# Five more pairs of projections as seven block products, between the heads of a hybrid decoder step

## The reference

```python
h = rmsnorm(x, norm1_w)
proj = jnp.einsum('btd,de->bte', h, w_in)
u_pool, u_qkv, b_raw, a_raw, z, gate_pool, gate_delta = jnp.split(proj, SPLITS, axis=-1)
y_pool, pool_buf_new = pool_mix(u_pool, pool_buf, pos0, w_pool, pool_scale)
qkv, conv_buf_new = causal_conv(u_qkv, conv_buf, w_conv)      # conv_buf_new: last 3 rows of u_qkv
# in gated_delta_chunked, for each head and chunk:
decay = jnp.exp(jnp.where(causal, G[..., :, None] - G[..., None, :], -jnp.inf))
A = jnp.einsum('bnhid,bnhjd->bnhij', kb, k) * decay * strict
t_inv = lax.linalg.triangular_solve(eye + A, ...)              # unit lower triangular
a_qk = jnp.einsum('bnhid,bnhjd->bnhij', q, k) * decay
# and after it:
o = rmsnorm(o, o_norm_w) * jax.nn.silu(z)
merged = jax.nn.sigmoid(gate_pool) * branch_pool + jax.nn.sigmoid(gate_delta) * branch_delta
```

## Time and profile before

| | |
|---|---|
| median of 3 runs | 568.15 us (567.43 to 569.66) |
| the profiled execution | 569.31 us, of which its span 567.5 us |
| TensorE busy | 528.8 us (93%) |
| VectorE, ScalarE, GpSimd busy | 291.0 (51%), 155.6 (27%), 166.1 us (29%) |
| HBM traffic | 277 GB/s over the span; 419 to 424 GB/s from about 370 to 540 us |

### The profile page before, as it was taken

How to read it: one execution, slowest core, us unless ns; L and a number is a source line. 1 busy time by engine, 2 the same in 40 slices (tenths; PEclk the granted TensorE clock), 3 DMA queues, 4 the chain that set the end, 5 groups by cost and what they waited for, 6 DMA issues and landing times.

```text
span 567.5 us, 13134 instructions
## 1 busy us (share of the span) xinstructions
PE 528.8 (93%) x5276; PEld 409.9 (72%) x5276; DVE 291.0 (51%) x843; ACT 155.6 (27%) x415; POOL 166.1 (29%) x247
## 2 busy tenths in 40 slices
PE   7999999999999999999999999999999949699983
PEld 6899999977777787998899888657455425365442
DVE  3877667683645848456756344533524411405044
ACT  3258466414862012233100124210011101010114
POOL 6687678113051199644033222000000000000001
PEclk9999999999999999999999999999999969889999
DMA  9835454566982138694479898899999999999992
GB/s 264 238 102 155 147 162 150 180 208 230 319 226 79 11 99 264 195 304 131 154 236 366 335 423 314 345 424 419 421 419 420 419 422 422 419 419 422 422 364 86
DMA packets 81375, 158.03 MB, mean 278 GB/s; under 512 B 11182, under 2 KB 65083, under 8 KB 69251
## 3 DMA queue, kind: packets, MB, share of 16 engines
q1 hardware_dynamic: 76572, 153.56, 73.7%
q10 hardware_dynamic: 4743, 3.64, 2.5%
HBM read 149.40 MB, written 7.96 MB: 277 GB/s over the span
## 4 chain that ended last, share of the span: by engine, by line
PE 73%; DMA 11%; SPq 6%; DVE 4%; issue 4%; ACT 1%; ACTq 0%; DVEq 0%
PE ps L1552 14%; PE ps L1545 12%; DMA arena<-in_w_up_dram 8%; PE ps L1874 6%; PE ps L2265 5%; PE ps L2119 5%; PE ps L2071 5%; SPq L733 4%; PE ps L2175 3%; PE ps L1498 3%; PE ps L2326 3%; PE ps L2026 2%; DMA arena<-in_w_down_dram 2%; PE ps L2346 2%; PE ps L2172 1%
## 5 line engine op out<-in xcount | busy, mean ns | idle before, releaser
L1545 PE MATMUL ps<-arena 128*128 128x288 f32 x320 | 81.4, 409 | 0.7 <-DVE arena L2516 0.7
L1552 PE MATMUL ps<-arena 128*128 128x144 f32 x616 | 78.3, 287 | 0.0
L1552 PEld LDWEIGHTS ps<-arena 128*128 128x128 f32 x616 | 76.3, 190 | 2.4 <-issue 1.9
L2265 PE MATMUL ps<-arena 128*32 128x256 f32 x1024 | 63.1, 403 | 14.8 <-DMA arena<-in_w_up_dram 13.0
L1545 PEld LDWEIGHTS ps<-arena 128*128 128x128 f32 x320 | 59.7, 190 | 17.2 <-issue 1.7
L2265 PEld LDWEIGHTS ps<-arena 128*32 128x32 f32 x1024 | 36.6, 116 | 39.3 <-issue 23.0
L997 POOL TENSOR_TENSOR arena<-arena 128x512 f32<-128x512 f32 x2 | 2.5, 1274 | 204.4 <-ACT arena L1458 204.4
L2541 DVE SCALAR_TENSOR_TENSOR ps<-arena,ps 128x312 f32<-128x312 f32 x72 | 39.1, 545 | 2.2 <-ACT ps L1117 0.9
L1874 PE MATMUL ps<-arena 128*128 128x144 f32 x280 | 37.0, 290 | 0.3 <-issue 0.3
L1874 PEld LDWEIGHTS ps<-arena 128*128 128x128 f32 x280 | 34.9, 190 | 1.7 <-issue 1.4
L1498 PE MATMUL ps<-arena 128*128 128x128 f32 (+7 forms) x162 | 26.7, 284 | 7.2 <-DVE arena L3320 5.1
(11 more groups left out here) (453 smaller groups left out, 844.1 us busy)
## 6 DMA issues: line engine op xcount, KB each, us to landing
arena<-in_w_gate_dram SPq DMA_DIRECT2D x32, 1024.0 KB, 12.5
arena<-in_w_up_dram SPq DMA_DIRECT2D x32, 1024.0 KB, 17.7
arena<-in_w_down_dram SPq DMA_DIRECT2D x28, 1024.0 KB, 17.8
arena<-in_w_in_dram SPq DMA_DIRECT2D x26, 1024.0 KB, 5.7
out_dram<-arena SPq DMA_DIRECT2D x9, 512.0 KB, 5.3
arena<-in_w_branch_delta_dram SPq DMA_DIRECT2D x4, 1024.0 KB, 10.4
arena<-in_w_out_dram SPq DMA_DIRECT2D x4, 1024.0 KB, 5.4
arena<-in_state_delta_dram SPq DMA_DIRECT2D x7, 512.0 KB, 8.2
```

What stands on the lines that cost most here:

```text
L1545: last = mm(ps[n % 2][:, 0:T], w[:, k, P * (n % 2):P * (n % 2) + P], hT[:, k, :], start=(k == 0), stop=(k == KD - 1))
L1552: last = mm(to[:, 0:HT], left[:, k, :], right[:, k, :], start=(first and k == 0), stop=(k == HK - 1), skip_group_check=True)
L2265: last = mm(to[CAP * e:CAP * e + CAP, 0:FE], xgT[:, k, CAP * e:CAP * e + CAP], w[e][:, k, :], start=(k == 0), stop=(k == KD - 1))
```

## The change

- Items 15 to 18 (PREP_PAIRS) and 19 (LAST_PREP) are computed in blocks too. Between the heads TensorE does four blocks of a pair, `prep(h)`, three blocks, `prep(h + 1)`; the sample's small products are moved to the places that the diff shows. Only items 14 and 20 stay plain.
- VectorE's `prep` is cut into `prep_times`, `prep_decays` and `prep_products`, with the additions of the pair between them. Three additions of item 19 stand inside the substitution; `new_values` stands ahead of it.
- ScalarE evacuates z with Copy and takes one Silu over all of zT later. It makes the spread columns of the second set (`second_columns`) and copies the sums of the tokens for the last five pairs (`token_sums`) from those made at the start, which lie in gT; VectorE's `sum_tokens` goes. `rows_exp(0)` stands ahead of the copy of the pool rows.
- GpSimd sums the weights of the five new pairs, and of LEAD_PAIR, in halves; the first of them ahead of the clearing of X.
- SP: the decay rows are stored and read back ahead of the conv stores. Both are tied to item 17, which now goes to slot 0, as item 18 did. PAIR_A is loaded inside `diagonal_blocks`.
- Slots, semaphore counts and the buffers of the last stage are renumbered accordingly.

The diff, cut to its core:

```diff
-LATE_FAST = range(IN_ITEMS - 5, IN_ITEMS)
-LEAD_PAIR, PAIR_A, PAIR_B, PAIR_C, PAIR_D = LATE_FAST
+PLAIN = IN_ITEMS - 6
+PREP_PAIRS = range(PLAIN - 5, PLAIN - 1)
+LAST_PREP = PLAIN - 1
+LATE_FAST = (*PREP_PAIRS, LAST_PREP, *range(PLAIN + 1, IN_ITEMS))
...
-SLOT_OF = [i % 4 if i < NQKV // 2 else i % RA for i in range(LATE_FAST[0])] + [3, 4, 1, 2, 3, 1, 2, 4, 3, 0, 5, 1, 2, 4, 3]
-LATE_SUMMED, LATE_SUMS = 0, 5
+SLOT_OF = [i % 4 for i in range(NQKV // 2)] + [0, 1, 2, 3, 4, 0, 1, 2, 3, 4, 5, 2, 3, 4, 2, 3, 5, 4, 1, 0, 2, 3, 5, 4]
+LATE_SUMMED, PREP_SUMS, LATE_SUMS = 1, 5, 0
+SUMS_ORDER = (*FAST, *PREP_PAIRS, LEAD_PAIR, LAST_PREP, PAIR_A, PAIR_B, PAIR_C, PAIR_D)
...
-CONV_AT = NQKV // 2 + RA
-ROWS_AT = NQKV // 2 + RA
-DIAG_AT = LATE_FAST[1]
+CONV_AT = NQKV // 2 + RA - 1
+ROWS_AT = NQKV // 2 + RA - 1
+DIAG_AT = LEAD_PAIR
...
+                load_weights(PAIR_A)
...
-                if i == RA + 15:
+                if i == RA + 13:
                     sp.wait_ge(S["memsets"], 1)
                     sp.dma_start(x_image, X[:, 0:2 * H * TILE]).then_inc(S["diag"], 16)
+                if i == ROWS_AT:
+                    head_rows()
                 if i == CONV_AT:
                     store_conv()
...
+                behind = i in LATE_FAST and i not in (PREP_PAIRS[0], LEAD_PAIR)
+                if behind:
+                    pool.wait_ge(S["proj"], product(pair_ahead(i), L_P7))
+                elif i in LATE_FAST:
+                    s, v = item_read(reader_ahead(i, sums_slot(i)))
                     pool.wait_ge(s, v)
-                elif i in LATE_FAST:
-                    pool.wait_ge(S["proj"], product(i - 1, L_P7))
                 if i - 2 in FAST:
                     pool.wait_ge(S["proj"], product(i - 2, P4))
-                nc.gpsimd.tensor_tensor(s1, a21, a22, ALU.add).then_inc(S["pads"], 1)
+
+                def combine(to, a, b, op):
+                    if i in PREP_PAIRS or i in (LAST_PREP, LEAD_PAIR):
+                        link(nc.gpsimd.tensor_tensor(to[:, 0:2], a[:, 0:2], b[:, 0:2], op))
+                        to, a, b = to[:, 2:HK], a[:, 2:HK], b[:, 2:HK]
+                    nc.gpsimd.tensor_tensor(to, a, b, op).then_inc(S["pads"], 1)
+
+                combine(s1, a21, a22, ALU.add)
                 pool.wait_ge(S["pads"], weights_summed(i, 1))
-                nc.gpsimd.tensor_tensor(s2, s1, a11, ALU.subtract).then_inc(S["pads"], 1)
-                nc.gpsimd.tensor_tensor(s3, a11, a21, ALU.subtract).then_inc(S["pads"], 1)
+                combine(s2, s1, a11, ALU.subtract)
+                combine(s3, a11, a21, ALU.subtract)
                 pool.wait_ge(S["pads"], weights_summed(i, 2))
-                if i in LATE_FAST[1:]:
-                    pool.wait_ge(S["proj"], product(i - 1, L_P3))
-                nc.gpsimd.tensor_tensor(s4, a12, s2, ALU.subtract).then_inc(S["pads"], 1)
+                if behind:
+                    pool.wait_ge(S["proj"], product(pair_ahead(i), L_P3))
+                combine(s4, a12, s2, ALU.subtract)
...
+            sum_weights(PREP_PAIRS[0])
             nc.gpsimd.memset(X, 0.0).then_inc(S["memsets"], 1)
...
+            sum_weights(PREP_PAIRS[1])
             pool.wait_ge(S["diag"], 16)
             own_columns(0)
-            pool.wait_ge(S["sd_pe"], 1)
-            own_columns(1)
-            sum_weights(LATE_FAST[0])
+            sum_weights(PREP_PAIRS[2])
+            sum_weights(PREP_PAIRS[3])
+            sum_weights(LEAD_PAIR)
+            sum_weights(LAST_PREP)
...
-                    nc.scalar.activation(zT[:, n - N_Z, :], src[:, 0:T], ACT.Silu).then_inc(S["proj_free"], 1)
+                    nc.scalar.activation(zT[:, n - N_Z, :], src[:, 0:T], ACT.Copy).then_inc(S["proj_free"], 1)
...
+            rows_exp(0)
             act.wait_ge(S["stage_out"], 16 * 2 * (1 + BD))
...
+            for i in PREP_PAIRS:
+                h = 2 * (i - PREP_PAIRS[0])
+                late_first(i)
+                if h:
+                    rows_exp(h)
+                rows_exp(h + 1)
+                if h == 4:
+                    second_columns()
+                if h == 0:
                     act.wait_ge(S["decdve"], 1)
                     nc.scalar.activation(Dq, Dq, ACT.Exp).then_inc(S["dec_act"], 1)
-                evac(N_Z + Z_AHEAD + h)
-            evac(N_Z + Z_AHEAD + H)
+            act.wait_ge(S["sums"], late_added(PREP_PAIRS[2], L_SUM1))
+            nc.scalar.activation(zT, zT, ACT.Silu).then_inc(S["silu"], 1)
+            late_first(LAST_PREP)
             act.wait_ge(S["diag"], 16 * IMAGE_WRITES)
             for m in BY_SCALAR:
                 read_diagonal(act, m)
-            for n in range(N_GATE + 3, N_GATE + LEAD_GATES):
-                if n == N_GATE + LEAD_GATES - 1:
-                    act.wait_ge(S["sub_done"], 1)
-                    for m in BY_SCALAR:
-                        write_inverse(act, m)
-                evac(n)
+
...
+                act.wait_ge(S["proj"], product(PREP_PAIRS[3], L_P2))
+                at = HT * (3 * HK + 2)
+                flat_sums = summed.rearrange("p j k t -> p (j k t)")
+                nc.scalar.activation(room_l[:, 0:at], flat_sums[:, 0:at], ACT.Copy).then_inc(S["ht_done"], 1)
+                nc.scalar.activation(room_w, flat_sums[:, at:], ACT.Copy).then_inc(S["ht_done"], 1)
+
+            token_sums()
+            late_tanh(PREP_PAIRS[3])
+            late_tanh(LAST_PREP)
+            evac(2 * PLAIN)
+            evac(2 * PLAIN + 1)
+            late_first(LEAD_PAIR)
+            act.wait_ge(S["sub_done"], 1)
+            for m in BY_SCALAR:
+                write_inverse(act, m)
...
+            def late_products(i, between=nothing):
+
+                a11, a12, a22 = late_left(i)
+                s1, s2, s3, s4 = [weight_sums(i)[:, j] for j in range(4)]
+                behind_plain = i in (PREP_PAIRS[0], LEAD_PAIR)
+                pe.wait_ge(ring_in[SLOT_OF[i]], 16 * loads_in(SLOT_OF[i], i + 1))
+                if behind_plain:
+                    pe.wait_ge(S["proj_free"], free[2 * i - 2])
+                else:
+                    pe.wait_ge(S["sums"], late_added(pair_ahead(i), L_SUM1))
+                late_block(0, a11, lambda k: hT[:, k, 0:HT])
+                between()
+                pe.wait_ge(S["pads"], weights_summed(i, 2))
+                if behind_plain:
+                    pe.wait_ge(S["proj_free"], free[2 * i - 1])
+                if i == LEAD_PAIR:
+                    pe.wait_ge(S["ht_done"], late_summed_by(2))
+                late_block(1, s2, late_right(i, 1))
+                pe.wait_ge(S["proj_free"], late_free(i, 1))
+                late_block(0, s1, late_right(i, 0))
+                pe.wait_ge(S["pads"], weights_summed(i, 3))
+                pe.wait_ge(S["sums"], late_added(i, L_SUM2))
+                late_block(1, s3, late_right(i, 2))
+
+            def late_products_back(i):
+
+                a11, a12, a22 = late_left(i)
+                s4 = weight_sums(i)[:, 3]
+                pe.wait_ge(S["pads"], weights_summed(i, 4))
+                pe.wait_ge(S["sums"], late_added(i, L_SUM4))
+                late_block(0, s4, lambda k: hT[:, HK + k, HT:T], opens=False)
+                pe.wait_ge(S["sums"], late_added(i, L_SUM7))
+                late_block(1, a22, late_right(i, 3), opens=False)
+                pe.wait_ge(S["sums"], late_added(i, L_SUM5))
+                late_block(0, a12, lambda k: hT[:, HK + k, 0:HT])
...
-            for h in range(H):
-                proj(N_Z + Z_AHEAD + h)
+            for i in PREP_PAIRS:
+                h = 2 * (i - PREP_PAIRS[0])
+                late_products(i)
                 prep(h)
                 if h == 0:
                     sample_rows()
-                if h == 2:
+                if h == 4:
                     sample_tiles(2, 0, TS, Nq, lambda own, j: ident[own, own])
-                if h == 3:
+                    state_products(0)
+                if h == 6:
+                    sample_tiles(4, 0, TS, IAq, lambda own, j: N2q[own, j, :])
+                late_products_back(i)
+                prep(h + 1)
+                if h == 4:
                     sample_tiles(3, 2 * TS, TS, tq, lambda own, j: Nq[own, j, :])
-                if h == 4:
-                    sample_tiles(4, 0, TS, IAq, lambda own, j: N2q[own, j, :])
-                    state_products(0)
-                if h == 5:
+                if h == 6:
                     sample_flips()
-            proj(N_Z + Z_AHEAD + H)
             state_products(1)
-
-
-            for n in range(N_GATE + 3, N_GATE + LEAD_GATES):
-                proj(n)
-                if n == N_GATE + 3:
-                    sample_tiles(7, 0, P, TTq, lambda own, j: Rq[own, j, :])
-                if n == N_GATE + LEAD_GATES - 1:
-                    sample_tiles(8, 2 * P, P, aqq, lambda own, j: vnq[own, j, :])
+            late_products(LAST_PREP)
+            sample_tiles(7, 0, P, TTq, lambda own, j: Rq[own, j, :])
```

(50 more changed lines are left out.)

182 lines of the change are left out of this document (78 added, 104 removed).

## The result

The changed kernel takes 578.81 us, the median of four runs (575.27 to 580.00), against 568.22 (567.43 to 569.66) for the kernel before in the same session: 1.0173 of it (95% interval 1.0121 to 1.0225). So it is some 10 us slower. In a later session the same kernel took 577.05 us (574.62 to 578.87, four runs), 1.0132 of before (1.0091 to 1.0172), some 8 us. The forecast was 571.3, with a range to 575.5; slower was the likelier sign by a hair (0.47 against 0.46 for no change), and the size is outside in both sessions.

The account below looks back on a forecast made before the run. TensorE bounds the kernel to about 355 us, then expert weight loads, so front changes carry through. -4.0 - 0.5 + 3.1 + 2.1 + 2.3 = +3.0, +3.1 with semaphores, gave 571.3 us; range 567.2 to 575.5.

Parts of the forecast that it names:

- the decay rows ahead of the conv stores: Front: rows' store, landing and reads (2.53 us) delay the pool rows' copy; first block +3.1 us later (2.5 to 5.2).
- The windows: VectorE's windows ahead of head 0's exponentials, held by GpSimd's sums, end at about 133.9 instead of 131.14.
- the 1.8 us of the row of the copy: The moved memset may hold the windows' additions 1.8 us more; taken as nothing, left in the range.
- The clock: Rival: TensorE's 3 us standstill at 134 halves its clock, losing 2.0 us: 573.3; chance 0.19 shared with VectorE's loop.
- Seven products between the heads: Loop of the heads: VectorE's two-input steps, held by GpSimd's sums, cost +2.1 us in all (0.3 to 4.5).
- The saving: Five pairs in blocks of half width instead of plain on TensorE: 0.8 us each, -4.0 us (3.5 to 4.5).
- The rival in which the additions hide: VectorE's and GpSimd's instructions slip past each other in gaps; loop loses only 0.3 us; 568.0, not slower; chance 0.24.
- the one in which each held step costs 0.64 more: Rival: VectorE bounds the loop of the heads; with the memset's 1.8 us, 575.5; chance 0.19 shared with the clock.
- The rival in which nothing waits at the conv stores: Pool rows' copy doesn't follow the last conv store, so the 3.1 us go: 565.1 to 568; chance 0.07.
- Behind the last head: After the last head's products, TensorE waits for VectorE's additions inside the substitution: +2.3 us (1.0 to 3.5).
- the ended waits: TensorE's waits at 197.08 and just after, behind the substitution, end as new values move ahead: -0.5 us at most.
- The range's lower end: Whole kernel: 567.2 us, said to come from the lower ends of queue and loop together.

Follow-up runs that it names:

- rows_by_scalar: Changed kernel, decay rows stored and read back from ScalarE's DMA queue, head 0's exponentials behind the pool rows: 572.01 us, 1.0038 of the kernel before.
- no_sums: As rows_by_scalar, but GpSimd's weight sums of six pairs are made on 8 columns of one block only: 569.83 us, single run.
- combined: As rows_by_scalar, with PAIR_B's load moved ahead of the inverse's write-back and head 0's exponentials behind the first product's copy: 567.38 us, 0.9973 of the kernel before.
- rows_ahead_of_load: Changed kernel, SP stores and reads the decay rows one item earlier, ahead of item 17's load: 573.96 us, 1.0092 of the kernel before.
- whole_sums: As rows_by_scalar, but each GpSimd sum is one 128 x 512 instruction, not two halves: 574.98 us, 1.0093 of the kernel before.
- before_rows_first: Kernel before, with only the decay rows stored and read back ahead of the conv stores: 579.15 us, 1.0187 of the kernel before.
- exp_behind: Changed kernel, only head 0's exponentials on ScalarE moved behind the pool rows: 577.54 us, 1.0148 of the kernel before.
- after_again: Changed kernel unaltered, run once more for a second profile, which is of a run of 578.87 us.

## Why the prediction was wrong

**The failed step: the decay rows ahead of the conv stores.** The mechanism was right: the copy of the pool rows follows the last conv store, there is no slack, and TensorE stands idle ahead of the third pool product. The size was not: +3.1 was forecast, 5.2 at most, and it was +6.8 in the first profile and 6.95 in the second. The step took store, landing and reads as 2.53 us from where they stood, and moved that price along. But there the store followed the conv stores, 18 KB each, and landed after 1.70; in its new place it follows a 1 MB load on the same queue. Copy to copy it is 138.76 less 131.92, less the 1.05 of the later start: 5.79, of which 2.53 were counted and 3.26 are the landing. The other 1.01 is the pool's product at half the clock. The Trainium skill (DMA: Bandwidth & Descriptors, Queues, rings and completion order) says that an engine takes the descriptors of one issuer's ring in order and alternates between rings. By it a small store behind a large load on SP's ring waits for that load; the landings of 4.9 and 6.8 behind loads against 2.4 without one agree. That a store on ScalarE's ring would not wait isn't shown: in rows_by_scalar it landed after 2.5, but it was issued at 114.21, ahead of that load.

**The windows** were a second bound in that step, and set too high. They were to end at 133.9; they ended at 133.41 in after, 132.36 without the later start. The moved memset ran beside the additions for 0.8 us and didn't hold them:

```profile
128.85 1.80 POOL L905 MEMSET arena<- 128x2048 f32 x1
129.85 2.47 DVE L2790 TENSOR_TENSOR arena<-arena 128x422 f32<-128x422 f32 x4
```

In no_sums the four additions take 2.48 with GpSimd idle. So the 1.8 us of the row of the copy were rightly left out of the sum. The rule of the Trainium skill that was weighed there (SBUF — State Buffer, Who interferes with whom), that a VectorE instruction with two SBUF inputs doesn't contend with a GpSimd instruction that only writes, agrees; the rows of copies that a memset did hold are of another kind of instruction.

**The clock.** It was a rival, priced at 2.0 and left out of the sum, and it came true. It cost 1.01 at the pool's product, inside the 6.8, and 1.39 in the first four blocks (5.47, against 4.08 in combined). The gap was 5.66 us where 3 were forecast; whether one of 3 would have done it no run shows, but one of 3.55 did, and so did four of the six waits of 1.80 to 2.11 us told of above. The Trainium skill (TensorE: Matmul & The Clock Gate, Part 1) has the fall follow from idleness and the return from work; the gaps of 3.55 us and more, and the 3 to 5 us of half speed behind them (3.1 in rows_ahead_of_load, 4.9 in after), agree.

**Seven products between the heads.** +2.1 was forecast for contention; no_sums and rows_by_scalar give 2.58. The four pairs and the flips' departure would have made the loop 42.59 - 3.2 - 0.9 + 2.1 = 40.6; after has 41.54 with the 1.39 of the clock in it, combined 40.72. The saving itself came as forecast: four blocks take 4.08, 1.02 each. Half a sum took 0.76 us (30.5 for 40), where 0.64 was estimated. The rival in which the additions hide falls with the steps of 643 ns in place of 419; the one in which each held step costs 0.64 more is near what whole_sums shows, and with halves it didn't come. The rival in which nothing waits at the conv stores falls with the row of L1204.

**Behind the last head.** +2.3 was forecast, 1.0 to 3.5. From the last head's products to `inner_y(0)` after has 28.49 against 26.81; without the moved block (1.02) and the flips (0.9), with the saved 0.8 and 0.5 added back, that is 1.1, in combined 1.5. These rows of after answer: the diagonal blocks land at 193.41, the third sum is made at 196.70, and the plain projection waits for it. LEAD_PAIR's 56 passes follow without a gap.

```profile
193.41 0.29 DVE L2993 TENSOR_SCALAR arena<-arena 128x256 f32<-128x256 f32 x1 [0.20 <-DMA arena<-a_image]
...
196.70 0.30 DVE L2888 TENSOR_TENSOR arena<-arena,ps 128x144 f32<-128x144 f32 x1
...
197.15 4.12 PE L1607 MATMUL ps<-arena 128*128 128x288 f32 x16 [1.03 <-DVE arena L2888]
...
205.75 7.04 PE L1828 MATMUL ps<-arena 128*128 128x144 f32 x56
```

Forecast was 0.95 for the fifth pair's last block and 1.3 for the plain pair. The first was 0.20 in after, at the weight load (0.42 in rows_by_scalar), and the second was 1.03.

**The sum without the front** was 0.0, with the saving, the ended waits, the loop and this stretch. Measured, first block to `inner_y(0)`, it is 70.03 - 69.40 - 1.02 - 1.39 = -1.8 in after and 69.66 - 69.40 - 1.02 = -0.8 in combined. The rest of the sum was good to 2 us, then, and it erred to the slow side. The range's lower end, 567.2, doesn't follow from the terms named for it: the lower ends of queue and loop take 0.6 and 1.8 from 571.3, which leaves 568.9. Nothing measured hangs on it.

**What was not in it at all** is the wait for instructions. The row of 0.73 us stood in the trace of before, but no edit of the change touches that place; still, with the changed program it is 1.8 to 2.1 in six of the seven profiles that leave PAIR_B's load where it was, and in four of them the clock falls behind it. Why it is longer there stays open. With the clock it makes 3.6 us, about as much as the 3.5 by which the first median lies above the first profile. The front's 6.8 and 1.4 and these 3.6, less the 0.73 that before waits there too and less the 1.8 of the rest, make 9.3 us, of the 9.6 by which the spans of before and of the second profile differ. Counted from the forecast, the front is 3.7 more than its term, the clock behind it 1.4, this wait 2.9, and the rest 1.8 less: 571.3 + 6.2 = 577.5, where the two medians are 578.81 and 577.05. The front's error alone would have ended inside the range.

## What to carry to other kernels

A small DMA has no price of its own: take its landing from a place with the same transfers ahead of it on the same queue, and where a short store or a wait for its landing moves, ask first what large load was issued just before. If another engine is idle and can issue it ahead of that load, issue it there. Where many short instructions run in a row, a large load issued at that moment can delay their instructions, and so can cost more than it brings.

## What the runs showed of the hardware

- The landing of the same 16 KB store took 1.7 (before), 2.4 (rows_ahead_of_load), 4.9 (after) and 6.8 us (before_rows_first), by what stood ahead on its queue.
- TensorE can stand for its own instructions. In nine profiles it has a wait of 0.26 to 2.11 us in `inner_xx`, which ends 2.4 to 2.7 us after a 16 KB packet of instructions starts on the DMA engines; that the packet holds the instructions it waits for is inferred from this. The Trainium skill (Advanced Engine Details and Errata, ISA Cache) gives lines of 16 KB for 256 instructions; 64 products with their weight loads are half a line, an estimate from that page, so that short products use up lines fast. No run shows what a packet holds.
- A gap in TensorE's work of 1.82 to 1.91 us brought the clock down in four profiles (exp_behind, rows_ahead_of_load, whole_sums, after_again); gaps of 1.80 (rows_by_scalar) and 2.11 us (no_sums) didn't. Gaps of 0.73 (before), 1.03 (before_rows_first) and 1.40 us (after, at 164.57) didn't; those of 3.55 to 7.54 us ahead of the pool's product did in all six profiles that have one.
- In whole_sums a 32 x 32 copy on VectorE, 0.17 us otherwise, was held for 2.94: until the last whole sum on GpSimd and the memset of 1.80 us behind it were done.
